# Attention preparation in steps within the last RWKV pair, and that pair's tail in steps within the attention

## The reference, cut to what matters

```python
h = rms_norm(x, norm_in_g[l])
p = h @ w_in[l]
y_rwkv = rwkv7_group(p_rwkv, ...)       # 8 heads of 64
y_nsa = nsa_group(p_nsa, pos, ...)      # 4 heads, three branches
y_mem = memory_group(p_mem, mem_k, mem_v, ...)   # 4 heads over 256 memory rows
x = x + concatenate([y_rwkv, y_nsa, y_mem]) @ w_out[l]
```

## Time and profile before

| What | us |
|---|---|
| median of three runs | 2870.28 (2870.10 to 2871.41) |
| the profiled execution | 2871.48 |
| its span | 2869.7 |
| RWKV's barrier of pair 3 | about 717.4 |
| first score of the attention | 785.07 |
| attention over | about 1018 |

### The profile page before, as it was taken

How to read it: one execution, slowest core, us unless ns; L and a number is a source line. 1 busy time by engine, 2 the same in 40 slices (tenths; PEclk the granted TensorE clock), 3 DMA queues, 4 the chain that set the end, 5 groups by cost and what they waited for, 6 DMA issues and landing times. The chain is left out here.

```text
span 2869.7 us, 42316 instructions
## 1 busy us (share of the span) xinstructions
PE 2574.7 (90%) x18624; PEld 1671.8 (58%) x18624; DVE 771.5 (27%) x1528; ACT 532.5 (19%) x1075; POOL 584.0 (20%) x367
## 2 busy tenths in 40 slices
PE   4899977887799998799998987999999999999991
PEld 4788856677576654688885553444544544544440
DVE  2311015554345423323222333111111111111114
ACT  2011123443255412111110320000000000000001
POOL 2433333331121111423330002111111111111103
PEclk9999979999699999899999987999989999999995
DMA  3122211000310011211113107999999999999984
GB/s 153 63 99 89 88 77 40 14 22 19 138 46 1 1 66 64 90 52 37 53 51 151 70 30 293 384 400 406 394 400 403 396 393 405 392 399 398 394 337 188
DMA packets 85887, 537.84 MB, mean 187 GB/s; under 512 B 13193, under 2 KB 13449, under 8 KB 43329
## 3 DMA queue, kind: packets, MB, share of 16 engines
q1 hardware_dynamic: 67728, 492.18, 43.4%
q10 hardware_dynamic: 7728, 26.06, 2.5%
q0 software_dynamic: 10240, 16.82, 1.6%
HBM read 503.54 MB, written 43.52 MB: 191 GB/s over the span
## 5 line engine op out<-in xcount | busy, mean ns | idle before, releaser
L218 PE MATMUL banks<-arena 64*64 64x64 f32 (+11 forms) x15392 | 1885.2, 364 | 151.8 <-issue 21.6
L218 PEld LDWEIGHTS banks<-arena 64*64 64x64 f32 (+3 forms) x15392 | 1098.1, 167 | 882.6 <-issue 723.0
L228 ACT ACTIVATE arena<-banks 128x512 f32<-128x512 f32 (+6 forms) x382 | 220.0, 586 | 1236.1 <-PE banks L218 599.8
L2574 POOL DMA_INDIRECT yb<-arena x64 | 65.1, 1018 | 911.5 <-DVE arena L2678 883.6
L223 PE MATMUL banks<-r,w2s 128*128 128x512 f32 x448 | 177.4, 396 | 19.1 <-POOL w2s L1955 19.1
L223 PE MATMUL banks<-r,wlo 128*128 128x512 f32 x432 | 171.3, 397 | 7.2 <-POOL wlo L404 7.2
L2687 DVE COPY arena<-banks 128x512 f32<-128x512 f32 x64 | 44.3, 692 | 489.3 <-PE banks L218 489.3
L224 PE MATMUL banks<-r,w2s 128*128 128x512 f32 x448 | 175.3, 391 | 0.0
L225 PE MATMUL banks<-r,w2s 128*128 128x512 f32 x448 | 175.0, 391 | 0.0
L225 PE MATMUL banks<-r,wlo 128*128 128x512 f32 x432 | 170.0, 394 | 0.0
L224 PE MATMUL banks<-r,wlo 128*128 128x512 f32 x432 | 169.8, 393 | 0.0
(11 more groups left out here) (242 smaller groups left out, 1570.6 us busy)
## 6 DMA issues: line engine op xcount, KB each, us to landing
arena<-in_wg SPq DMA_DIRECT2D x64, 2048.0 KB, 9.7
arena<-in_wu SPq DMA_DIRECT2D x64, 2048.0 KB, 14.4
arena<-in_wd SPq DMA_DIRECT2D x64, 2048.0 KB, 18.6
arena<-in_w SPq DMA_DIRECT2D x55, 512.0 KB, 3.5
spill<-arena SPq DMA_DIRECT2D x27, 512.0 KB, 2.6
arena<-spill SPq DMA_DIRECT2D x22, 512.0 KB, 4.9
arena<-yb SPq DMA_DIRECT2D x8, 1024.0 KB, 13.0
arena<-in_x SPq DMA_DIRECT2D x12, 512.0 KB, 4.8
```

The source lines that it names most:

```text
L218: return pe.e.matmul(o, l, r, start=start, stop=stop)
L228: return act.e.activation(o, i, ACT.Copy)
L2574: return pool.e.indirect_dma_start(yb, bass.IndirectOffsetOnAxis(ap=six[:, col:col + 1].bitcast(U32), axis=0), src[:, :], None, bounds_che ...
```

## The change

The preparation becomes a third kind of side step, N, in pair 3's main part: `SIDE` is now a list, one string for each pair. Its tiles are laid where pair 2's buffers and the prologue's scratch lie, so its loads wait for pair 2's end. Only q0, q1, the keys, `kvc`, `cw1`, `rope` and the masks are loaded there, all by SP; the masks come as bf16 bits from the host, so the conversion on POOL is gone; small weights are loaded by ACT before the RWKV stage. The compression's products alternate between the two halves of rows and share one bank. The preparation's own barrier is gone. After the RWKV barrier SP issues both key swaps, the loads of m0, m1 and the gates, and, once the last tail is over, all of w_out. The tail of pair 3 is taken in two steps in each turn of the attention, so it is over after turn 10; its products use bank 3 alone (ring "last"), and the scores of units 0 to 15 the banks 0 to 2 (ring "score3"). DVE scales m0 and m1 at the end of turn 0, ACT turns the gates at the end of turn 4. Tiles that the tail uses are moved within the arena and within `yT`.

```diff
+        self.rings = {..., "side": (6, 7), "score3": (0, 1, 2), "last": (3,)}
...
     def sp_rwkv(sp):
...
+        sp_nsa_load(sp)
         sp.wait_ge(s("y_done"), NP - 1)
         load(gq[:, :], G0 + NP - 1, "g_load")
...
     def pe_tail(pe, i):
+        ring = "side" if i < NP - 1 else "last"
...
-    SIDE = "TT" + "PT" * 12 + "T" * 9
-
-    def run_rwkv(eng, prologue, main, tail, last):
+    SIDE = ["TT" + "PT" * 12 + "T" * 9] * (NP - 1) + ["T" * 8 + "NT" * 8 + "T" * 20]
+
+    def run_rwkv(eng, prologue, main, tail, nsa):
...
         for i in range(NP):
-            side = {"T": tail(eng, i - 1) if i else iter(()), "P": prologue(eng, i + 1) if i < NP - 1 else iter(())}
-            order = iter(SIDE)
+            side = {"T": tail(eng, i - 1) if i else iter(()), "P": prologue(eng, i + 1) if i < NP - 1 else iter(()),
+                    "N": nsa(eng) if i == NP - 1 else iter(())}
+            order = iter(SIDE[i])
...
         end_rwkv(eng)
-        tail3 = tail(eng, NP - 1)
-        for _ in range(12):
-            next(tail3)
-        interleave(1, tail3, last(eng))
...
     def sp_nsa_load(sp):
+
+        for name in ("B", "K", "D", "R"):
+            sp.wait_ge(s(name), NP)
+        wait_main(sp, NP - 2)
         tl_load(sp, 5)
+        sp.e.dma_start(cw1[:, :, :], inp["cw1"]).then_inc(s("cmp_weights").sem, 16)
+        tl_load(sp, 0, 1)
         sp.e.dma_start(rope[:, :, :], inp["rope"]).then_inc(s("rope").sem, 16)
+        tl_load(sp, 4)
+        sp.e.dma_start(ambits[:, :], inp["amask"]).then_inc(s("mask_load").sem, 16)
+
+    def sp_attention(sp):
         sp.wait_ge(s("rope_k"), 2)
         sp.e.dma_start(kx[64:128, :], kr[0:64, :]).then_inc(s("k_swapped").sem, 16)
+        sp.e.dma_start(kx[0:64, :], kr[64:128, :]).then_inc(s("k_swapped").sem, 16)
+        tl_load(sp, 2, 3, 6, 7, 8, 9)
+
+        sp.wait_ge(s("y_done"), NP)
+        for c in range(8):
+            sp.e.dma_start(wo[:, c, :], inp["wo"][c * 128:(c + 1) * 128, :]).then_inc(s(f"wo{c}").sem, 16)
...
     def pe_nsa(pe):
...
+        u = ps.open(pe, "cmp_hid", hold=True, ring="side")
+        for j in range(32):
+            for lo in (0, 64):
+                hs = slice(lo, lo + 64)
                 mm(pe, u.t[hs, 0:63], cw1[hs, j, :], kvc[hs, j:j + 16 * 62 + 1:16], j == 0, j == 31)
+            if j == 15:
+                yield
...
     def dve_nsa(dve):
...
+        yield
+        dve_scale_q(dve, 0)
+        dve_scale_q(dve, 1)
+        yield
...
     def pe_scores(pe, u, it):
...
+        ring = "score3" if u < 16 else "score"
+        if br == 3:
+            pe.wait_ge(s("q_scaled"), 4)
...
     def pe_attention(pe):
-        pe.wait_ge(s("mask_cast"), 1)
+        tail3 = pe_tail(pe, NP - 1)
+        pe.wait_ge(s("mask_load"), 16)
         pe.wait_ge(s("k_swapped"), 32)
...
             if its:
                 pe_scores(pe, v, 0)
+            next(tail3, None)
...
             if len(its) == 2:
                 pe_scores(pe, v, 1)
+            next(tail3, None)
...
     def dve_attention(dve):
...
+            next(tail3, None)
+            if v == 0:
+                dve_scale_q(dve, 2)
+                dve_scale_q(dve, 3)
...
     def act_attention(act):
...
+            if v == 4:
+                for c in range(4):
+                    act.wait_ge(s(f"tl{6 + c}"), 16)
+                    act.e.activation(gates[c][:, :], gates[c][:, :], ACT.Silu).then_inc(s("gates").sem, 1)
...
         run_rwkv(pe, pe_prologue, pe_main, pe_tail, pe_nsa)
-        end_nsa(pe)
         pe_attention(pe)
```

More of the change, by code:

```diff
@@ L121, in __init__ @@
         self.count, self.table, self.next, self.held = [0] * len(self.tiles), {}, 0, {}
-        self.rings = {"score": (0, 1, 2, 3), "turn": (4, 5), "o": (6, 7), "main": (0, 2, 4), "side": (6, 7), "nsa": (0, 1, 2, 3, 4)}
+        self.rings = {"score": (0, 1, 2, 3), "turn": (4, 5), "o": (6, 7), "main": (0, 2, 4), "side": (6, 7), "score3": (0, 1, 2),
+                      "last": (3,)}
         self.turn = {ring: 0 for ring in self.rings}
@@ L1092, in pe_tail @@
             S = Hm[i % 2][:, 0, :] if c == 1 else Sm[:, c % 2, :]
-            u = ps.open(pe, ("state", i, c), ring="side")
+            u = ps.open(pe, ("state", i, c), ring=ring)
             if c < 15:
@@ L1200, in run_rwkv @@
                 next(side[which], None)
-            for which in "PT":
+            for which in "NPT":
                 for _ in side[which]:
@@ L1228, in program @@
-    qr = [sb(f"qr{i}", [128, T], c=c3_) for i in range(2)]
[L1229 to L1238, removed]
-    cw1 = sb("cw1", [128, 32, 64], c=prep)
@@ L1240, in program @@
-    assert edge[0] <= at_tail
-    prep.close()
-    q0, q1, m0_, m1_, ksw, kvc = tl[:6]
-    gates = tl[6:]
-    high = Scope(1)
-    small = sb("small", [128, 64], c=high)
-    woc = Scope(1)
-    wo = sb("wo", [128, 8, D], c=woc)
-    rtmp = [sb(f"rtmp{i}", [128, 512], c=woc) for i in range(3)]
-    amb = sb("amb", [128, NAM], BF16, c=woc)
-    Pb = {br: sb(f"P{br}", [128, 2, 2, w], c=c3_) for br, w in ((1, 1024), (3, 256), (2, 640), (0, 64))}
-    PT = [sb(f"PT{i}", [128, 2, 2, 128], c=c3_) for i in range(4)]
+    q0, q1, kr, kx = (sb(n, [128, T], c=c3_) for n in ("q0", "q1", "kr", "kx"))
@@ new lines, in program @@
+    qr = [sb(f"qr{i}", [128, T], c=c3_) for i in range(2)]
+    ambits = sb("ambits", [128, NAM // 2], c=c3_)
+    amb = ambits.bitcast(BF16)
+    at_prep = edge[0]
+    kvc, ksw = (sb(n, [128, T], c=c3_) for n in ("kvc", "ksw"))
+    cw1 = sb("cw1", [128, 32, 64], c=c3_)
+    rope = sb("rope", [128, 2, T], c=c3_)
+    rtmp = [sb(f"rtmp{i}", [128, 512], c=c3_) for i in range(2)]
+    assert edge[0] <= at_last
+    after_prep = edge[0]
+    m0_, m1_ = (sb(n, [128, T], c=c3_) for n in ("m0_", "m1_"))
@@ L1253, in program @@
+    gates = [sb(f"gate{n}", [128, T], c=c3_) for n in range(4)]
+    tl = [q0, q1, m0_, m1_, ksw, kvc, *gates]
+    Pb = {br: sb(f"P{br}", [128, 2, 2, w], c=c3_) for br, w in ((3, 256), (2, 640), (0, 64))}
     Dg = [sb(f"Dg{i}", [128, 4, 128], c=c3_) for i in range(3)]
@@ L1258, in program @@
     nm = sb("nm", [128, 8, 8], c=c3_)
+    assert edge[0] <= at_tail
+    after_attention, edge[0] = edge[0], at_prep
+    Pb[1] = sb("P1", [128, 2, 2, 1024], c=c3_)
+    PT = [sb(f"PT{i}", [128, 2, 2, 128], c=c3_) for i in range(4)]
+    assert edge[0] <= after_prep
+    edge[0] = after_attention
+    high = Scope(1)
+    small = sb("small", [128, 64], c=high)
+    woc = Scope(1)
+    wo = sb("wo", [128, 8, D], c=woc)
     c3_.close()
@@ L1341, in act_nsa @@
         act.e.activation(g4[:, :, :, 0:3], vtok[:, :, 128:140].rearrange("p j (h b) -> p j h b", h=4), ACT.Sigmoid).then_inc(s("g4").sem, 1)
-        yield
-        yield
-        yield
-        act.wait_ge(s("rope_k"), 2)
-        act.e.dma_start(kx[0:64, :], kr[64:128, :]).then_inc(s("k_swapped").sem, 16)
-        for c in range(4):
-            act.wait_ge(s(f"tl{6 + c}"), 16)
-            act.e.activation(gates[c][:, :], gates[c][:, :], ACT.Silu).then_inc(s("gates").sem, 1)
+        for _ in range(4):
+            yield
     def dve_nsa(dve):
-        for _ in range(2 * 12 + 2):
-            yield
         dve.e.memset(g4[:, :, :, :], 1.0).then_inc(s("gate_ready").sem, 1)
```

204 lines of the change are left out of this document (95 added, 109 removed).

## The result

The changed kernel takes 2856.57 us (median of 7 runs, 2849.78 to 2861.50), the kernel before 2870.10 beside it (7 runs, 2868.82 to 2871.41). The ratio is 0.995 with an interval of 0.9939 to 0.9962: faster, by 13.5 us where 33.7 were forecast; the time itself lies near the upper end of the range (2858). In this series the changed kernel's runs scatter over 11.7 us, the others' over 2.6; in the series of the experiments the kernel before scatters over 11 to 15 us as well, so a wider scatter is not shown to be the change's.

A forecast was written before the change was run, and what follows sets the result against it. It took a serial 67.7 us stage between pair 3 and the attention as the removable cost: -67.7 + 14.5 + 4.5 + 2 + 10 + 5 + 2 - 2 - 2 = -33.7, from 2870.28 to 2836.6 us; range 2820 to 2858.

The forecast's parts named there:

- Removed, 67.7 us: Between pair 3's main part and the attention: the serial stage from 717.4 to 785.07 us goes whole, -67.7 us.
- N in the main part, +14.5: Pair 3's main part: eight preparation steps add 13.7 us of PE work plus about 5%; +14.5 us, bounds 9 and 22.
- The loads, 0 "hidden by steps 1 to 8": Pair 3's main part: loads feeding N land by about 660 us, before step 9 needs them; 0 us.
- The wait for the swap, +4.5: Before the first turn: both key swaps wait for the RWKV barrier, nothing covers them; +4.5 us, bounds 3.7 to 9.
- Score banks, +2: Units 0 to 15: three score banks instead of four, PE usually having other products between items; +2 us.
- the rival's 46: Units 0 to 15: three banks lock PE to ACT, each of 24 items losing 2 us, 48 in all; chance 0.06.
- The tail, +10: Turns 0 to 10: pair 3's tail beside the attention, priced from earlier pairs; +10 us, bounds 8.3 and 11.5.
- ACT's lumps, +5: First turns: three lumps of ACT work with table loads, 13.6 us, partly reach PE; +5 us, bounds 0 and 13.6.
- The clock, -2: First turns: entered from clock 0.97 after 4.5 us, so less time at half clock; -2 us, bounds -8 and +5.
- the clock stays down: Rival: turns 0 to 10 run mostly at half clock, 15 us on top, 2852 us; chance 0.08.
- 5 + 2 - 2 - 2: First turns: ACT's lumps +5, three score banks +2, ACT no longer issuing w_out's loads -2, the clock -2 us.
- ACT's lumps in full: Rival: in the first turns ACT's lumps reach PE whole, adding 8.6 us to the 5, 2845 us; chance 0.13.

The follow-up runs named there:

- e_loads_late: Against the changed kernel: N steps run alone behind pair 3's main part, their loads issued only when that part is over; 2870.35 us, ratio 0.9977.

## Why the prediction was right and wrong

**Removed, 67.7 us: right.** All of it is gone, and the stages behind the attention only shifted (1877.2 us from the last diagonal to the end of the span before, 1878.1 after).

**N in the main part, +14.5: 14.4, and partly by luck.** The compression cost 10.0 where 7.2 stood, the rest 4.4 where 7.3 did; the two errors cancel. I had halved the 0.11 us a record of the earlier trace rows twice, once for the full clock and once for the two halves side by side. For the products of 64x1 both came: 0.029 us a record at full clock. For those of 64x63 only one of the two halvings did. From 666.9 to 674.0 us, with the clock at 1.00, a record of them starts every 0.054 us, as in nearly all these kernels; their 128 records are busy 7.3 us where my price makes 3.6. In e_loads_late such products, alone on PE, passed from one clock level to the other and started every 0.054 us on both sides (a window also counts the records that reach over its edge):

```profile
730.20:733.10 2.90, 2.90 (x54) 2.90 (x56) 1.16 (x2) 0.00 (x0) 0.00 (x0) 0.50 1.04 431
733.10:737.10 4.00, 4.00 (x79) 4.00 (x77) 0.23 (x1) 0.00 (x0) 1.93 (x1) 1.00 0.91 372
```

So the alternation seems to have brought its half (one half alone took 0.109 at 0.50) and the full clock nothing; why is open.

**The loads, 0 "hidden by steps 1 to 8": this step failed.** I asked only whether they land in time. They do; no wait of PE for kvc or cw1 shows. But 4.5 MB beside a stage made of thousands of small instructions cost it 6 us, PE getting through 300 records where it did 427. In the kernel before, the loads stood beside the tail's latency chain, where it could not be seen. With some 2 us for the tail's order ("its work is the same: 0"; within the scatter) and 2 open ones, among which the lower clock, this makes the 10 us that the main part is over my figure.

**The wait for the swap, +4.5: 5.8 us.** Right in kind, a DMA ends it, and within the bounds.

**Score banks, +2: mis-sized, 7.0.** My bounds went from 0 up to the rival's 46. The rival's mechanism is real: PE waits for Exp item by item. Its place was right, its price too high by far: seven waits of 16.8 us in the first eleven turns, of which 7.0 us are lost.

**The tail, +10: 6.4 as counted**, at unlike clocks, as told above, so that a miss of my 8.3 to 11.5 is not shown. It fills waits that the banks make: PE waits 8.3 to 9.4 us for Exp with it and 16.8 without. **ACT's lumps, +5:** the gates' is worth 3.8, and 5.6 us of wait in the kernel with the tail alone; the others were not tried alone. **m0 and m1, +2:** 1.7 us of wait.

**The clock, -2: wrong sign.** I expected turns entered from 0.97 after 4.5 us of idleness to start warm. The changed kernel fell to half clock inside that wait and stayed there as long as the kernel before did behind its 10.4 us, first after, then before:

```profile
742.00:762.40 20.40, 13.25 (x100) 9.86 (x100) 6.92 (x26) 6.45 (x22) 2.08 (x2) 0.50 0.49 172
```

```profile
777.90:798.40 20.50, 8.80 (x50) 7.07 (x52) 5.03 (x14) 11.41 (x27) 2.08 (x2) 0.50 0.64 231
```

The turns run at 0.79 to 0.83, below the 0.84 of before, with 9 to 15 us more at half clock by the windows, and the main part at 0.85 to 0.90 for 0.97, with 14 to 24 us more. With levels of one to two at most half of such a time is lost, by estimate up to 5 to 7 us in the turns, so this is the rival "the clock stays down" in part: it put 15 us into the turns alone. Two profiles of the changed kernel differ by 3.8 us in the main part with clocks of 0.85 and 0.90; the scatter of the whole has other sources too, as pair 3 starts anywhere between 647.4 and 659.4 us in kernels that are the same up to there.

In sum, over the forecast: loads 6, order and rest of the main part 4, banks 5, swap 1.3, and the turns with four banks and no tail 7.7 (10.7 where 5 + 2 - 2 - 2 stood), less the tail's 3.6: 20.4 of the missing 20.2 us. That it closes is no proof, since these are steps of one chain of kernels from 50.3 and 64.8 us to 74.4 and 89.4. Of the 10.7 us 5.7 are PE's work at the lower clock and 5.0 waits, the gates' lump first.

Of the signs I had named, the 5.9 us that a DMA ends and the table loads in the turns came; the main part's stretch (91.0 for 77 to 82), the way from the first score to unit 10's diagonal (75.8 for 66) and the clock of 0.9 did not.

The rival "ACT's lumps in full" does not hold for the gates' lump: leaving it out gave 3.8 of its 6.5 us. The trace has 1.28 us a table load; ACT's work ends 0.01 us before the one at 773.37 and goes on 0.02 us behind it, and two loads fewer changed nothing that shows. The Trainium skill, ScalarE: Activation LUTs, What ACT_TABLE_LOAD costs, has 1283 ns for the load, which the trace confirms, and some 1380 ns of drain on top, which no row here shows.

## What to carry to other kernels

A load that lands in time is not free when it runs beside an engine that works through small instructions by the thousand: count what else uses the DMA queues, the instruction fetches above all. When work is moved into a stage, look at what the move takes from it besides time, here one of four PSUM banks: that cost about as much as the work. And issue the DMA that the next stage waits for before the barrier between the stages, if its data are ready by then; it is the cheapest edit of all here. A price read at one clock must not be halved for the other without a row that shows it.

## What the runs showed of the hardware

PE's instructions come as 16 KB packets on a DMA queue of their own, mostly one for each 3.5 to 4.8 us of the RWKV main part, and 6.4 us lie between two of them beside 4.65 MB of loads. Products of 64x1 in alternating halves took 0.029 us a record at full clock; products of 64x63 took 0.054, at a clock of 1.00 and of 0.50 alike (one half alone at 0.50: 0.109). The kernel before had a median of 2870 us in one series and 2871 to 2875 in the others (2868.65 to 2884.51), so that only ratios taken side by side can be compared.
